# Other orders of tiles, splits, squares and first weights in the feed-forward sublayers of a hybrid decoder step

## What is computed

```
def rmsnorm(x, g):
    xf = x.astype(jnp.float32)
    y = xf * lax.rsqrt(jnp.mean(xf * xf, axis=-1, keepdims=True) + EPS) * g.astype(jnp.float32)
    return y.astype(x.dtype)

def swiglu(h, w_gate, w_up, w_down):
    return (jax.nn.silu(h @ w_gate) * (h @ w_up)) @ w_down
...
        x = x + 0.5 * rmsnorm(swiglu(rmsnorm(x, ng[0]), p['w_ffn_gate'][i, 0],
                                     p['w_ffn_up'][i, 0], p['w_ffn_down'][i, 0]), ng[1])
        h = rmsnorm(x, ng[2])
...
        x = x + rmsnorm(y, ng[3])
        x = x + 0.5 * rmsnorm(swiglu(rmsnorm(x, ng[4]), p['w_ffn_gate'][i, 1],
                                     p['w_ffn_up'][i, 1], p['w_ffn_down'][i, 1]), ng[5])
```

## Time and profile before

| | us |
|---|---|
| median of the runs (2485.8 to 2612.95) | 2488.42 |
| the profiled execution | 2487.07 |
| its span on the core | 2485.3 |
| PE busy | 2332.6 (94%) |
| DVE busy | 1627.3 (65%) |
| POOL busy | 1107.6 (45%) |
| ACT busy | 1070.9 (43%) |
| mean granted clock of PE | 0.975 of full speed |

### The profile page before, as it was taken

How to read it: one execution, slowest core, us unless ns; L and a number is a source line. 1 busy time by engine, 2 the same in 40 slices (tenths; PEclk the granted TensorE clock), 3 DMA queues, 4 the chain that set the end, 5 groups by cost and what they waited for, 6 DMA issues and landing times. The chain is left out here.

```text
span 2485.3 us, 45038 instructions
## 1 busy us (share of the span) xinstructions
PE 2332.6 (94%) x17619; PEld 2237.7 (90%) x17619; DVE 1627.3 (65%) x3004; ACT 1070.9 (43%) x2192; POOL 1107.6 (45%) x841
## 2 busy tenths in 40 slices
PE   7899999689999998999997899999999998899998
PEld 6899998589999988999986898888987987899997
DVE  5685584768585676765845666758567438686585
ACT  4353343334343453443446455363452224353343
POOL 2565562046565626655632022241223642665562
PEclk9999999899999999999999999999999999999999
DMA  3233323013333312332322434425445341233322
GB/s 121 63 104 98 102 82 104 20 43 100 114 104 109 96 59 79 106 97 86 99 75 63 112 84 120 126 59 133 127 118 146 101 158 61 73 94 98 103 81 75
DMA packets 294604, 235.57 MB, mean 95 GB/s; under 512 B 37339, under 2 KB 284788, under 8 KB 294107
## 3 DMA queue, kind: packets, MB, share of 16 engines
q1 hardware_dynamic: 294395, 232.71, 30.8%
HBM read 207.20 MB, written 27.93 MB: 95 GB/s over the span
## 5 line engine op out<-in xcount | busy, mean ns | idle before, releaser
L886 POOL TENSOR_TENSOR w_l<-raw,w_h 128x512 fp32r<-128x512 f32 (+1 forms) x416 | 522.1, 1275 | 330.9 <-ACT w_h L1635 330.9
L886 POOL TENSOR_TENSOR w_l<-wsum,w_h 128x512 fp32r<-128x512 f32 x216 | 332.6, 1548 | 364.3 <-ACT w_h L1635 364.3
L1146 PE MATMUL acc<-hid,w_h 128*128 128x272 f32 x2432 | 461.2, 288 | 8.4 <-DVE y L2243 8.4
L1635 ACT ACTIVATE w_h<-raw 128x512 fp32r<-128x512 f32 (+1 forms) x576 | 323.3, 585 | 166.2 <-PE acc L1146 113.7
L1146 PEld LDWEIGHTS acc<-hid,w_h 128*128 128x128 f32 x2432 | 382.8, 188 | 10.7 <-issue 10.7
L1146 PE MATMUL acc<-hid,w_l 128*128 128x272 f32 x1216 | 349.4, 287 | 0.0
L2245 DVE TENSOR_TENSOR y<-acc,y 128x272 f32<-128x272 f32 x192 | 84.7, 441 | 253.6 <-PE acc L1146 230.9
L1635 ACT ACTIVATE w_h<-wsum 128x512 fp32r<-128x512 f32 x216 | 134.9, 625 | 259.6 <-DVE wsum L2180 243.9
L1146 PEld LDWEIGHTS acc<-hid,w_l 128*128 128x128 f32 x1216 | 228.9, 188 | 0.0
L1344 PE MATMUL acc<-hhi,dhi 128*128 128x272 f32 (+1 forms) x1040 | 197.4, 311 | 13.0 <-POOL hlo L1022 3.7
L1685 ACT ACTIVATE hid<-hidf 128x272 fp32r<-128x272 f32 x176 | 75.2, 427 | 293.4 <-DVE hidf L2368 192.5
(11 more groups left out here) (334 smaller groups left out, 6153.0 us busy)
## 6 DMA issues: line engine op xcount, KB each, us to landing
raw<-in_w_ffn_gate_dram SPq DMA_DIRECT2D x44, 1024.0 KB, 5.1
raw<-in_w_ffn_up_dram SPq DMA_DIRECT2D x44, 1024.0 KB, 5.1
raw<-in_w_ffn_down_dram SPq DMA_DIRECT2D x48, 768.0 KB, 4.4
wraw<-in_dn_w_in_dram SPq DMA_DIRECT2D x48, 512.0 KB, 4.0
raw<-in_w_ffn_down_dram SPq DMA_DIRECT2D x16, 512.0 KB, 3.3
room<-in_state_delta_dram SPq DMA_DIRECT2D x16, 512.0 KB, 4.8
out_delta_sample_dram<-room SPq DMA_DIRECT2D x16, 512.0 KB, 4.2
wraw<-in_dn_w_out_dram SPq DMA_DIRECT2D x16, 512.0 KB, 5.1
```

The source lines that it names most:

```text
L886: pool.tensor_tensor(w_l[o % RING][:, 0:n, :], source(step, i), w_h[o % RING][:, 0:n, :].bitcast(F), ALU.subtract)\
L1146: last = pe.matmul(acc[m][:, hf, 0:HT], w[o % RING][:, k % HK4, :], hid[:, k, z, cols(hf)], start=(k == 0 and j == 0), stop=(k == step.til ...
L1635: act.activation(w_h[o % RING][:, 0:n, :], source(step, i), ACT.Copy).then_inc(op_hi, 1)
```

## The change

- Plain part on DVE: `normed` is cut in two halves of four, and the tiles of step 1, the differences 0 and 1 and the hidden splits are interleaved; in step 3 each split follows the next tile; `difference(2)` moves from ahead of step 3's tiles to behind its last split, and `difference(3)` goes to the other buffer and no longer waits for the third split.
- On POOL `low_difference(0)` and `(1)` move from behind step 2's weight splits to behind step 3's, and `(2)` from behind step 3's to behind step 4's. On ACT `high_difference(2)` and `high_quarter(0)` move between the hidden tiles of step 3 and the weights of step 5.
- Squares: those of the tiles 12 and 13 are added by PE instead of DVE; `add_late` for tile 11 follows that for 10 directly; the second half's `add_early` moves into `down_halves`.
- First weights: DVE splits only the two blocks of the first output tile, in one go; POOL splits the two of the second. In `first_gate` the high products of the second tile come before the low ones of the first.

The counters (`ADDS`, `low_counts`) follow.

```diff
--- before.py
+++ after.py
@@ -128,7 +128,7 @@
 
 
 def by_vector(step, i):
-    return i in (A11, A22) if step.seven else step is steps_of(step.e)[0]
+    return i in (A11, A22) if step.seven else step is steps_of(step.e)[0] and i < 2
 
 
 def low_counts():
@@ -142,8 +142,8 @@
                 pool += 1
             ops.append((by_vector(step, i), dve if by_vector(step, i) else pool))
         ends.append((pool, dve))
-        if at in (2, 3):
-            for _ in range(4 - at):
+        if at in (3, 4):
+            for _ in range(5 - at):
                 pool += 1
                 differences.append(pool)
     return ops, ends, differences
@@ -509,7 +509,7 @@
         H_LO = [0, None, 20, 40, 60, 76]
         AUX_PAST, AUX_PRODUCTS, AUX_TAIL, AUX_DN = 11, 13, 15, 17
         SUMS = [0, 2, 18, 20, 22, 24]
-        ADDS = [0, None, 10, 20, 30, 40]
+        ADDS = [0, None, 8, 16, 24, 34]
         X_ADDS = [0, None, 22, 44, None, 66]
         w_in = I["dn_w_in"].rearrange("l k n -> (l k) n")
         w_out = I["dn_w_out"].rearrange("l k n -> (l k) n")
@@ -896,10 +896,10 @@
                     for i in range(step.ops):
                         if not by_vector(step, i):
                             low_of(step, i)
-                    if step is steps[2]:
+                    if step is steps[3]:
                         low_difference(r, 0)
                         low_difference(r, 1)
-                    if step is steps[3]:
+                    if step is steps[4]:
                         low_difference(r, 2)
 
             def pool_mixer():
@@ -1037,7 +1037,7 @@
                 pe.matmul(aux[hf][:, 0:HT], ones_mean, squared(n), start=(mt == 0), stop=(mt == KT - 1)).then_inc(ss_done, 1)
 
             def add_early(r, hf):
-                pe.wait_ge(ss_add, ADDS[r] + ((9, 10) if r in (1, 4) else (8, 10))[hf])
+                pe.wait_ge(ss_add, ADDS[r] + ((9, 10) if r in (1, 4) else (8, 6))[hf])
                 pe.matmul(aux[hf][:, 0:HT], ones_mean, ssacc[:, hf, :], start=True, stop=False)
 
             def add_late(r, n):
@@ -1084,11 +1084,11 @@
                     products(0, hf, w_h, hhi, h_hi)
                     if hf == 0 and late is not None:
                         late()
-                    pe.wait_ge(*low_ready(a + 1))
-                    products(0, hf, w_l, hhi)
                     pe.wait_ge(op_hi, b + 2)
                     freed(1, hf)
                     products(1, hf, w_h, hhi)
+                    pe.wait_ge(*low_ready(a + 1))
+                    products(0, hf, w_l, hhi)
                     products(0, hf, w_h, hlo, h_lo)
                     pe.wait_ge(*low_ready(b + 1))
                     products(1, hf, w_l, hhi)
@@ -1169,15 +1169,15 @@
                                 add_early(r, 0)
                             if hf and mt == 4 and k == HK4 - 1:
                                 add_late(r, 10)
+                                add_late(r, 11)
                             if hf and mt == 5 and k == 1:
-                                add_late(r, 11)
+                                add_early(r, 1)
                         if hf == 0:
                             last.then_inc(res, 1)
 
             def sums_end(r):
-                add_early(r, 1)
-                add_late(r, 14)
-                add_late(r, 15)
+                for n in range(12, 16):
+                    add_late(r, n)
 
             def past_transposes():
                 pe.wait_ge(past_in, 32)
@@ -1694,7 +1694,7 @@
                         act.wait_ge(prod, steps[4].op)
                     elif n == 1:
                         act.wait_ge(x_add, X_ADDS[r] + 22)
-                    src = tf[:, 0] if n == 1 else y[:, ks, cols(hf)]
+                    src = tf[:, 1] if n == 1 else y[:, ks, cols(hf)]
                     act.activation(hhi[:, ks, cols(hf)], src, ACT.Copy).then_inc(h_hi, 1)
 
                 for i in range(2):
@@ -1718,12 +1718,12 @@
                     silu(steps[2], n, n // 2, n % 2)
                 for i in range(2):
                     round_op(steps[4], i)
-                high_difference(2)
                 for n in range(4):
                     hidden(steps[3], n, 2 * n + 2)
+                high_difference(2)
+                high_quarter(0)
                 for i in range(2):
                     round_op(steps[5], i)
-                high_quarter(0)
                 for step in steps[6:8]:
                     high_quarter(2 * (step.p - 2) + 1)
                     for i in range(2):
@@ -2163,8 +2163,8 @@
                 dve.wait_ge(op_hi, o + 1)
                 dve.tensor_tensor(w_l[o % RING][:, 0:n, :], source(step, i), w_h[o % RING][:, 0:n, :].bitcast(F), ALU.subtract).then_inc(lo_dve, 1)
 
-            def low_first(e, m):
-                for i in (2 * m, 2 * m + 1):
+            def low_first(e):
+                for i in range(2):
                     low_of(steps_of(e)[0], i)
 
             def weight_sums(step):
@@ -2200,7 +2200,7 @@
 
             def add_square(r, n):
                 mt, hf = TILES_F[n]
-                before = ADDS[r] + (n - 3 if n < 9 else 7 if n == 9 else (8 if n == 12 else 9))
+                before = ADDS[r] + (n - 3 if n < 9 else 7)
                 dve.wait_ge(y_sq, 16 * r + n + 1)
                 if mt == 1:
                     dve.tensor_tensor(ssacc[:, hf, :], squared(n - 2), squared(n), ALU.add).then_inc(ss_add, 1)
@@ -2249,10 +2249,6 @@
                     n = 12 + k // 2
                     mt, hf = TILES_F[n]
                     evict(steps_of(e)[-4 + mt // 2], mt % 2, hf)
-                    if k >= 4:
-                        add_square(r, n - 2)
-                    if k == 4 and e == 1:
-                        low_first(2, 0)
                 return between
 
             def ffn(e, r):
@@ -2282,18 +2278,18 @@
                     dve.tensor_tensor(hid[:, tile, 1, cols(hf)], hidf[:, s, :], hid[:, tile, 0, cols(hf)].bitcast(F), ALU.subtract)\
                        .then_inc(hid_lo, 1)
 
-                def normed(hf):
-                    for k in range(KT):
+                def normed(hf, ks):
+                    for k in ks:
                         dve.scalar_tensor_tensor(y[:, k, cols(hf)], x[:, k, cols(hf)], gain(r // 3, 2 * (r % 3), k), rpre[:, hf, :],
                                                  ALU.mult, ALU.mult).then_inc(x_add, 1)
 
                 def difference(n, a, b):
                     dve.wait_ge(x_add, X_ADDS[r] + 18 + n)
-                    dve.tensor_tensor(tf[:, n % 2 if n < 3 else 0], a, b, ALU.subtract).then_inc(x_add, 1)
+                    dve.tensor_tensor(tf[:, n % 2], a, b, ALU.subtract).then_inc(x_add, 1)
 
                 def low_quarter(n):
                     ks, hf = ((slice(0, HK4), 0), (slice(0, HK4), 1), (slice(HK4, KT), 1), (slice(HK4, KT), 0))[n]
-                    src = tf[:, 0] if n == 1 else y[:, ks, cols(hf)]
+                    src = tf[:, 1] if n == 1 else y[:, ks, cols(hf)]
                     dve.wait_ge(h_hi, H_HI[r] + 19 + n + 1)
                     dve.tensor_tensor(hlo[:, ks, cols(hf)], src, hhi[:, ks, cols(hf)].bitcast(F), ALU.subtract).then_inc(h_lo, 1)
 
@@ -2305,23 +2301,29 @@
                     dve.wait_ge(rb_ready, 4 * r + hf + 1)
                     for m in range(2):
                         plain_gate(steps[0], m, hf)
-                    normed(hf)
+                    normed(hf, range(0, HK4))
+                    if hf:
+                        plain_up(steps[1], 0, 0)
+                    normed(hf, range(HK4, KT))
+                plain_up(steps[1], 0, 1)
                 difference(0, b12, b11)
-                plain_up(steps[1], 0, 0)
+                hidden_low(steps[1], 0, 0)
+                plain_up(steps[1], 1, 0)
                 difference(1, b22, tf[:, 0])
-                for n in range(1, 4):
-                    plain_up(steps[1], n // 2, n % 2)
-                for n in range(4):
-                    hidden_low(steps[1], n, n)
+                hidden_low(steps[1], 1, 1)
+                plain_up(steps[1], 1, 1)
+                hidden_low(steps[1], 2, 2)
+                hidden_low(steps[1], 3, 3)
                 for n in range(4):
                     plain_gate(steps[2], n // 2, n % 2)
+                for n in range(4):
+                    plain_up(steps[3], n // 2, n % 2)
+                    if n:
+                        hidden_low(steps[3], n - 1, n - 1)
+                hidden_low(steps[3], 3, 3)
                 dve.wait_ge(lo_pool, LOW_DIFFERENCES[3 * e])
                 difference(2, b22, b12)
-                for n in range(4):
-                    plain_up(steps[3], n // 2, n % 2)
-                for n in range(4):
-                    hidden_low(steps[3], n, n)
-                dve.wait_ge(lo_pool, LOW_DIFFERENCES[3 * e + 2])
+                dve.wait_ge(lo_pool, LOW_DIFFERENCES[3 * e + 1])
                 difference(3, b21, tf[:, 1])
                 low_quarter(0)
```

(12 more changed lines are left out.)

## The result

The changed kernel takes 2454.36 us (median of five runs, 2452.82 to 2458.33) against 2488.42 us; the ratio is 0.986, 95% interval 0.985 to 0.987. The profiled execution fell from 2487.07 to 2452.82 us. One run of the kernel before, at 2612.95 us, was 5% slower than the rest and is left out of the ratio.

What follows compares the result with a forecast made beforehand. PE was taken as the bound, busy 94% of the span, leaving some 150 us idle plus clock loss. Plain part −18.5 and boundaries −12.6 made −31.1 us from 2487.07: 2456 us, with more than 8 in 10 between 2441 and 2469.

Steps and rivals of the forecast that it cites:

- the plain part with the down steps: Inside the four feed-forward sublayers: gaps removed, a longer wait at the second down step and its clock, −18.5 us in all.
- the boundaries: Kernel start, end and sublayer boundaries: moved sums of squares and first-weight splits together bring −12.6 us.
- The tiles' and the POOL gap: Plain part: PE's 1.45 us wait for DVE and 4.25 us wait for POOL go, with the clock's loss: −31.5 us.
- What is late next: Second down step: PE's gap grows to 3.5 us from 1.69, then 0.8 from 0.4; +8.6 us over four sublayers.
- The second gap: PE's further wait right behind the gap at the second down step: 0.8 us for 0.4.
- The clock behind the down gap: Behind PE's wait at the second down step: 2.2 us of clock loss in two of four sublayers, +4.4 us.
- The rival with no gap: Second down step: PE's wait does not grow and the clock stays up; −44 us, 2443 us; chance 16%.
- Squares: Ends of sublayers: post norm starts sooner; −4.0 us before the pooling mixer, −2.7 before the DeltaNet mixer, −2.7 at the end.
- First weights: First gates, splits shared by DVE and POOL: −1.9 us at the start, +2.5, −2.6, −1.2 before second, third, fourth sublayers.
- The pooling mixer's +2.5: Before the second sublayer: two POOL splits each hold up DVE's windows, which PE waits for, by about 1.25 us.
- the −1.2: Before the fourth sublayer: DVE drops a pair of splits, and its norm reads PSUM, which POOL does not delay.
- The slower rival: First seven-product step waits for weights whose load follows splits now behind `low_difference(2)`; at 10 us, 2496 us; chance 2%.

Runs made afterwards that it cites:

- early_differences: The changed kernel with `difference(2)` and `difference(3)` taken earlier on DVE, between the up tiles, and ACT's `high_difference(2)` after the second hidden tile: 2439.7 us, ratio 0.981.
- after_again: The changed kernel once more, unaltered, for a second profile: 2454.3 us, ratio 0.986.
- plain_only: The kernel before with the whole plain part changed (tiles and splits of differences), squares and first weights as before: 2474.3 us, ratio 0.995.
- plain_again: The kernel before with only the plain part changed, run once more unaltered for a second profile: 2474.1 us, ratio 0.993.
- gate_order_back: The changed kernel with the first gate's products in the old order, low products of the first tile ahead of high ones of the second: 2458.3 us, ratio 0.988.
- second_on_vector: The changed kernel with DVE again splitting all four blocks of the second feed-forward sublayer's first weights: 2449.8 us, ratio 0.986.

## Why the prediction was right, and where it was off

The forecast of 2456 us missed by 2 us, partly because errors of either sign cancel: the plain part with the down steps brought 24.4 us for 18.5, the boundaries 10.0 for 12.6. Two of its sums are also rounded off: 4 × (1.4 + 4.2 + 2.2) is 31.2, not 31.5, and 4 × 2.2 is 8.8, not 8.6, 0.5 us together.

*The tiles' and the POOL gap* (−31.5). Right in place and mechanism. Measured −33.3; the term that was small is the clock behind the 4.25 us gap: 2.2 us was read in the third sublayer and taken for all four, but the lost clock there was 3.1, 2.9, 2.3 and 1.7 us.

*What is late next* (+8.6). The chain was right: two differences on DVE, a quarter split in turns with POOL, the eviction, and the weight split behind POOL's `low_difference(2)`; early_differences shows that it is this chain. POOL's weight split ends it, 0.3 us behind the evictions (the prediction had 0.8 us between them), in a gap of 3.3 us for my 3.5. The second gap is 0 to 0.5 us for 0.8. The growth without the clock is 1.5 us per sublayer (second and fourth), not 2.2, and four times that 6.1 us, not 8.6.

*The clock behind the down gap* (+4.4, two of four). In the profile after it is two of four, and the lost clock there is 1.6 + 2.8 = 4.4 us. That is luck, and it is not what the falls cost: the two steps grew by 1.1 and 1.8 us more than those without a fall, 2.9 in all, in part because the slower PE waits less behind it (the second gap is 0.2 us and none, 0.5 without a fall). So 6.1 + 2.9 makes the table's 8.9 before rounding, and both terms were too large. Behind gaps of 3.27 to 3.31 us the clock fell in 18 of 24 places (kernels after, after_again, plain_only, plain_again, gate_order_back, second_on_vector), behind 3.75 us in 4 of 4, behind 4.25 us in 12 of 12, behind 0.5 us in 0 of 12. Three of four would have been the better count, at 0.8 to 2.0 us of time each, 1.5 on average over the 18. The rival with no gap came at 2443 us; the kernel in which that gap is taken away runs in 2439.7.

*Squares.* −4.0, −2.7 and −2.7 were right in place and nearly in size: −4.1, −2.7, −2.2 alone. At the third sublayer they bring the 2.6 to 3.1 us that I had put down to the first weights: the step that failed there is the one that closed PE's 2.60 us gap by DVE's dropped splits. Alone these shorten it by 1.2 us, to 1.41, and the splits that POOL took over are paid back in turns (5.44 us for 3.38). The earlier norm of the squares part shortens it by 1.6 us, to 0.96, with no such price. I had given the squares no gain at this boundary.

*First weights.* The start was −1.9 and is −3.3 in one profile, −1.8 in the other: the difference is a fall of the clock, which I had not priced. The pooling mixer's +2.5 is +2.0, shown by second_on_vector. At the fourth sublayer the −1.2 is there (PE's first products of the old wait come 1.2 us earlier), but slow clock took 2.2 us back: 0.7 in the first half, where the products that follow now run in a stretch at 1.2 GHz that was there before, and 1.5 by a fall in the second half.

*What I had not seen*: those falls in the second half of the first gates, 1.5 to 1.6 us each, behind a 0.95 us wait for ACT that was there before. In the profile after there are three. In the fourth sublayer all seven kernels with the new first weights have one and none of the six without; at the second and third it depends on no part that I could tell. So in the fourth it comes with the handover of the splits, not with the order of the products (gate_order_back has it too); how, and what decides it elsewhere, stays open.

*The slower rival* (the first seven-product step waits for its weights): no such wait in any trace.

## What to carry to other kernels

When a stall is taken away, follow the work that ran inside it to where it runs next: here two DVE instructions came to stand ahead of an eviction and of POOL work that a weight split waits behind, and putting them where DVE mostly waits anyway was worth another 12 to 15 us, more than a third of what the change gave. A gap of 3 us on PE should be priced with the clock behind it, here 1.5 us on average in three cases of four, and parts that each remove gaps need not add, since a gap that one part leaves can cost clock that it didn't cost before. A handover from DVE to POOL was paid back here where DVE's next work read two SBUF operands at the same time; where it read PSUM, at the fourth sublayer, it brought its 1.2 us, but slow clock took 2.2 us and that start came out 1 us longer all the same.

## What the runs showed of the hardware

- The clock behind one and the same gap is not fixed by the gap: 0.95 to 0.97 us in the first gate's second half cost nothing or 1.5 to 1.6 us, the down gap of 3.3 us nothing or 0.8 to 2.0 us. One program repeated its falls in a second profile, another did not.
- DVE and POOL in turns: eight splits of the input 5.44 us for 3.38, the large window addition 2.58 for 1.56, and an addition of 32 columns 1.13 for 0.19: that short instruction, from 443.18 on, ended at 444.31 with POOL's second split (444.26).
- The DeltaNet mixer, which no kernel here changes, took 782.5 us in the profile after and 787.5 in after_again, with nearly the same lost clock (26.4 and 26.6 us): an untouched stretch can hide or feign 5 us, more than most of the terms above.
